# Residual behind layers 1 to 3: two of four column groups turned by VectorE and in-SBUF transfers instead of TensorE

## What is computed

```python
for i in range(DEPTH):
    hn = rmsnorm(x, norm_g[i])
    y = mixer[i % 3](hn, w_in, ..., w_out)   # proj = h @ w_in ... o @ w_out
    x = x + y
return rmsnorm(x, final_g)
```

## Time and profile before

| | |
|---|---|
| runs | 1754.71, 1755.09, 1756.72 us |
| span of the profiled execution | 1753.0 us (the page gives no device time of that execution by itself; the span lies 2.1 us under the median run) |
| PE, matmuls | 1743.7 us busy, 99% |
| DVE | 1146.3 us, 65% |
| ACT | 912.2 us, 52% |
| DMA queue of SP | 64.5% of 16 engines |
| granted TensorE clock | 0.999 mean |
| adds of `xres`, groups 0 and 1 behind layer 1 | at 432.17 and 438.22 us of the span |
| the same behind layers 2, 3 and 4 | 761.07 and 767.12; 1228.19 and 1234.24; 1699.07 and 1705.12 us |

### The profile page before, as it was taken

The page is one execution under the profiler, slowest core; times in us unless marked ns, Lnnn a source line. Parts: engine busy times, 40 slices in busy tenths (PEclk is TensorE's granted clock), DMA queues, the critical chain, the costliest instruction groups (busy, mean ns, idle before and its releaser), DMA issues.

```text
span 1753.0 us, 25040 instructions
## 1 busy us (share of the span) xinstructions
PE 1743.7 (99%) x8282; PEld 1457.9 (83%) x8282; DVE 1146.3 (65%) x1902; ACT 912.2 (52%) x1424; POOL 40.2 (2%) x99
## 2 busy tenths in 40 slices
PE   9999999999999999999999999999999999999998
PEld 7888888888888888888888888888888888888887
DVE  7766666665558888865655565655666666666655
ACT  7554545454556666645544444454545445454543
POOL 1000000000000000000000000000000000000000
PEclk9999999999999999999999999999999999999999
DMA  8666565655565555457997699866566666656563
GB/s 281 180 179 180 169 183 173 183 167 192 181 185 164 159 156 156 152 180 166 170 164 209 175 166 179 210 172 189 182 188 175 178 178 174 184 169 181 171 212 131
DMA packets 171301, 313.16 MB, mean 179 GB/s; under 512 B 10871, under 2 KB 27837, under 8 KB 171101
## 3 DMA queue, kind: packets, MB, share of 16 engines
q1 hardware_dynamic: 170800, 311.54, 64.5%
q0 software_dynamic: 48, 0.13, 0.2%
q10 hardware_dynamic: 380, 0.56, 0.1%
HBM read 310.10 MB, written 2.10 MB: 178 GB/s over the span
## 4 chain that ended last, share of the span: by engine, by line
PE 99%; DMA 0%; issue 0%; DVE 0%; ACT 0%; SPq 0%; POOLq 0%; POOL 0%; DVEq 0%
PE acc L962 30%; PE acc L964 30%; PE acc L963 30%; PE tp L927 4%; PE sc L963 1%; PE sc L962 1%; PE sc L964 1%; PE sc L994 0%; DMA xres<-in_x_dram 0%; PE sc L1052 0%; PE sc L1050 0%; PE sc L1051 0%; PE sc L1033 0%; PE sc L1032 0%; PE tp L962 0%
## 5 line engine op out<-in xcount | busy, mean ns | idle before, releaser
L1781 DVE TENSOR_TENSOR w_lo<-raw,w_hi 128x1024 fp32r<-128x1024 f32 x583 | 707.8, 1223 | 457.4 <-ACT w_hi L899 456.1
L899 ACT ACTIVATE w_hi<-raw 128x1024 fp32r<-128x1024 f32 x583 | 613.5, 1059 | 451.1 <-PE acc L964 445.0
L962 PE MATMUL acc<-w_hi,xt_hi 128*128 128x512 f32 x1824 | 719.5, 394 | 0.0
L964 PE MATMUL acc<-w_hi,xt_lo 128*128 128x512 f32 x1824 | 711.4, 390 | 0.0
L963 PE MATMUL acc<-w_lo,xt_hi 128*128 128x512 f32 x1824 | 710.3, 389 | 0.0
L964 PEld LDWEIGHTS acc<-w_hi,xt_lo 128*128 128x128 f32 x1824 | 342.3, 188 | 72.6
L963 PEld LDWEIGHTS acc<-w_lo,xt_hi 128*128 128x128 f32 x1824 | 342.8, 188 | 65.8
L962 PEld LDWEIGHTS acc<-w_hi,xt_hi 128*128 128x128 f32 x1824 | 342.6, 188 | 65.6
L962 PE MATMUL acc<-w_hi,ot_hi 128*128 128x512 f32 (+1 forms) x520 | 202.5, 390 | 0.0
L964 PE MATMUL acc<-w_hi,ot_lo 128*128 128x512 f32 (+1 forms) x520 | 200.9, 386 | 0.0
L963 PE MATMUL acc<-w_lo,ot_hi 128*128 128x512 f32 (+1 forms) x520 | 200.7, 386 | 0.0
(11 more groups left out here) (289 smaller groups left out, 1145.6 us busy)
## 6 DMA issues: line engine op xcount, KB each, us to landing
raw<-in_da_w_in_dram SPq DMA_DIRECT2D x255, 512.0 KB, 3.7
raw<-in_ml_w_in_dram SPq DMA_DIRECT2D x96, 512.0 KB, 5.3
raw<-in_sw_w_in_dram SPq DMA_DIRECT2D x72, 512.0 KB, 3.7
raw<-in_da_w_out_dram SPq DMA_DIRECT2D x64, 512.0 KB, 3.7
raw<-in_sw_w_out_dram SPq DMA_DIRECT2D x32, 512.0 KB, 3.6
raw<-in_ml_w_in_dram SPq DMA_DIRECT2D x64, 256.0 KB, 4.8
raw<-in_ml_w_out_dram SPq DMA_DIRECT2D x32, 512.0 KB, 3.8
xres<-in_x_dram SPq DMA_DIRECT2D x3, 512.0 KB, 8.9
```

What stands on the lines that cost most here:

```text
L899: act.activation(w_hi[:, q:q + 2, :], raw[:, 2 * p:2 * p + 2, :], ACT.Copy).then_inc(hi_ready, 1)
L962: pe.matmul(out_ap, k_hi, m_hi, start=start, stop=False)
L964: return pe.matmul(out_ap, k_lo, m_hi, start=False, stop=stop)
L1781: dve.tensor_tensor(w_lo[:, two, :], raw[:, two, :], w_hi[:, q:q + 2, :].bitcast(F32), ALU.subtract).then_inc(lo_ready, 1)
```

## The change

For groups 0 and 1 behind layers 1 to 3 PE makes no transposes. DVE, right behind the add, transposes the group in blocks of 32x32 with one instruction (128x1024 elements). SP then moves each block to its place among the partitions: 16 transfers of 32 partitions x 1 KB for a group, four at each of four slots (22 to 25 for group 0, 24 to 27 for group 1), behind that slot's weight load, the first ones after a wait for the transpose. ACT and DVE split the group from SBUF at slots 24 and 26 instead of 20 and 22 from PSUM. Buffers `th`, `qs`, `gs` and part of `scr`, which stand idle there, are used. The table `X_SPLIT` holds for layer 4 too. Groups 2 and 3 and the start stay as they are.

```diff
-X_SUM, X_TURN, X_SPLIT, X_END = (18, 20, 27, 3), (16, 18, 25, 1), (20, 22, 29, 5), (14, 16, 24, 32)
+X_SUM, X_TURN, X_SPLIT, X_END = (18, 20, 27, 3), (16, 18, 25, 1), (24, 26, 29, 5), (14, 16, 24, 32)
+X_MOVE, X_MOVED = (22, 24), 2
...
+        x_blocks = [scr_flat[:, 4 * BLK:4 * BLK + T * JW].rearrange("p (t j n) -> p t j n", t=T, j=4),
+                    gs[:].rearrange("p t (j n) -> p t j n", j=4)]
+        x_moved = [th[:].rearrange("p t (j n) -> p t j n", j=4), qs[:].rearrange("p t (j n) -> p t j n", j=4)]
+
+        def x_chunk(n, c):
+            return (th, qs)[n][:].rearrange("p t (j k n) -> p (t j) k n", j=4, k=4)[:, :, c, :]
...
+            def move_x(l, idx):
+
+                for n in range(X_MOVED):
+                    q = idx - X_MOVE[n]
+                    if l == NL - 1 or not 0 <= q < 4:
+                        continue
+                    if q == 0:
+                        sp.wait_ge(sig["x_turned"], in_out(l, "x_turned", n + 1))
+                    for j in range(4):
+                        sp.dma_start(x_moved[n][32 * j:32 * j + 32, :, q, :], x_blocks[n][32 * q:32 * q + 32, :, j, :])\
+                          .then_inc(sig[f"x{n}_moved"], 16)
...
                     sp.dma_start(raw[:, 2 * s:2 * s + 2, :], rows_of[:, :, JW * n:JW * n + JW]).then_inc(raw_full[s], 16)
+                    move_x(l, q)
...
+                if l >= 0 and n < X_MOVED:
+                    act.wait_ge(sig[f"x{n}_moved"], in_out(l, f"x{n}_moved", 256))
+                    for c in range(4):
+                        at = KC * (l + 1) + 4 * n + c
+                        dst = xt_hi[:, 4 * n + c, :].rearrange("p (j n) -> p j n", n=32)
+                        act.activation(dst, x_chunk(n, c), ACT.Copy, scale=gcol[:, at:at + 1]).then_inc(sig["t_hi"], 1)
+                    return
...
                     if w.first_job_of_layer:
-                        pe.wait_ge(free[name], in_out(w.l - 1, name, 3 if p == 0 else 4))
+                        pe.wait_ge(sig["x_lo"], in_out(w.l - 1, "x_lo", X_MOVED))
+                        pe.wait_ge(free[name], in_out(w.l - 1, name, (3 if p == 0 else 4) - X_MOVED))
...
-                if (ln := w.x_due(X_TURN)) is not None:
+                if (ln := w.x_due(X_TURN)) is not None and ln[1] >= X_MOVED:
...
+                if l >= 0 and n < X_MOVED:
+                    dve.wait_ge(sig[f"x{n}_moved"], in_out(l, f"x{n}_moved", 256))
+                    for c in range(4):
+                        at = KC * (l + 1) + 4 * n + c
+                        lo, hi = (buf[:, 4 * n + c, :].rearrange("p (j n) -> p j n", n=32)
+                                  for buf in (xt_lo, xt_hi[:].bitcast(F32)))
+                        if c % 2 == 0:
+                            dve.wait_ge(sig["t_hi"], in_out(l, "t_hi", 4 * n + c + 2))
+                        op = dve.scalar_tensor_tensor(lo, x_chunk(n, c), gcol[:, at:at + 1], hi, ALU.mult, ALU.subtract)
+                    op.then_inc(sig["x_lo"], 1)
+                    return
...
+                if l < NL - 1 and n < X_MOVED:
+
+                    wait_emptied(dve, l, OUT0[l] + n)
+                    dve.transpose(x_blocks[n].rearrange("p t j (k n) -> p t k j n", n=32),
+                                  xres[:, :, JW * n:JW * n + JW].rearrange("p t (k j n) -> p t k j n", k=4, j=4))\
+                       .then_inc(sig["x_turned"], 1)
```

More of the change, by code:

```diff
@@ L79 @@
     "t_hi":      ((0, 0, 16), (0, 4, 16), (0, 2, 16), (0, 4, 16)),
+    "x_turned":  ((0, 0, 0), (0, 0, 2), (0, 0, 2), (0, 0, 2)),
+    "x0_moved":  ((0, 0, 0), (0, 0, 256), (0, 0, 256), (0, 0, 256)),
+    "x1_moved":  ((0, 0, 0), (0, 0, 256), (0, 0, 256), (0, 0, 256)),
+    "x_lo":      ((0, 0, 0), (0, 0, 2), (0, 0, 2), (0, 0, 2)),
     "x_sq":      ((0, 0, 8), (0, 0, 8), (0, 0, 8), (0, 0, 8)),
@@ L369, in build, with x_tp @@
         vs_row, gs_row = scr_flat[0:8], gs[0:8].rearrange("p t n -> p (t n)")
+        x_blocks = [scr_flat[:, 4 * BLK:4 * BLK + T * JW].rearrange("p (t j n) -> p t j n", t=T, j=4),
[3 more added lines that the diff above has]
+            return (th, qs)[n][:].rearrange("p t (j k n) -> p (t j) k n", j=4, k=4)[:, :, c, :]
+        def x_tp(l, n):
+            return in_out(l, "tp_0", n if l < 0 else n - X_MOVED), in_out(l, "tp_1", n if l < 0 else n - X_MOVED)
         RUN = T * (PAD + P)
@@ L653, in x_half_turned_hi @@
                 cols = [gcol[:, at + c2:at + c2 + 1] for c2 in range(2)]
-                turned_hi(lambda c: xt_hi[:, 4 * n + c, :], b, f"tp_{b}", in_out(l, f"tp_{b}", n), cols)
+                turned_hi(lambda c: xt_hi[:, 4 * n + c, :], b, f"tp_{b}", x_tp(l, n)[b], cols)
             act.dma_start(rows[0:64, :], norm_g.rearrange("l (c p) -> (l c) p", p=P)).then_inc(gains_in, 16)
@@ L944, in x_turn @@
             def x_turn(l, n):
-                if l < NL - 1:
-                    turn_eight(lambda t: xres[:, t, JW * n:JW * n + JW], [in_out(l, f"tp_{b}", n) for b in range(2)])
+                if l < NL - 1 and not (l >= 0 and n < X_MOVED):
+                    turn_eight(lambda t: xres[:, t, JW * n:JW * n + JW], x_tp(l, n))
             pe.wait_ge(consts, 1)
@@ L1335, in x_half_turned_lo @@
                 turned_lo(lambda c: xt_lo[:, 4 * n + c, :], lambda c: xt_hi[:, 4 * n + c, :].bitcast(F32), b, f"tp_{b}",
-                          in_out(l, f"tp_{b}", n), [gcol[:, at + c2:at + c2 + 1] for c2 in range(2)],
+                          x_tp(l, n)[b], [gcol[:, at + c2:at + c2 + 1] for c2 in range(2)],
                           in_out(l, "t_hi", 4 * n + 2 * b))
```

## The result

The changed kernel took 1766.69 us (median, 1766.14 to 1768.83), the kernel before 1755.14 beside it: ratio 1.0066, 95% interval 1.0054 to 1.0078. It is slower by 0.66%, where a gain of 5.4 us was forecast; 1766.7 lies above the range. The rival that came true is C, SP's run of issues, at a smaller size than it was priced, and with a second loss that no case of the prediction had.

What follows compares the result with a forecast made beforehand. PE was taken to bound the kernel, with the new chain hidden in ACT's and DVE's lead: six turns of 0.90 us, 5.4 us, off 1755.1 give 1749.7 us. Range 1748.8 to 1753.5 us.

Steps and rivals of the forecast that it cites:

- C: SP's 37 issues in a row behind each boundary become the bound from 0.56 us each; 1788 us at 0.87; chance 0.07.
- What bounds the kernel: PE, busy 99% of the span with two waits, both in the start; six turns removed at 0.90 us give 5.4 us.
- DVE's transpose: Right behind the add of slot 18: 1.23 us, hidden in DVE's idle time up to 2.45 us.
- splits from SBUF: ACT's splits of groups 0 and 1 at slots 24 and 26: 1.57 us each, against 1.55 from PSUM.
- the two final gains of layer 4: DVE at slots 24 and 26: 1.37 us each, less than its 1.50 us wait for ACT per slot, cost 0.
- I take 0.48: SP's run from slot 22 on: issues start 0.48 us apart, so group 1's last move is issued at 452.1.
- 1.1 us to spare: Slot 27 behind layer 1, the tightest place: `w_lo` ready at 464.8, PE wants it at 465.9.
- Landing: Moves land 3.7 us after issue, like weight loads: group 0 at 449.1, group 1 at 455.8.
- The lead: ACT and DVE are 5.6 us ahead of PE's need at each slot; 4.5 of it is used.
- The clock: PE around the turns kept for groups 2 and 3: granted clock stays 1.00, the 2.4 GHz level, with no idle PE.
- B: Blocks come late at the three boundaries and part of the gain is given back: 1752.3 or 1753.9 us; chance 0.14.
- Rival D: PE's matmuls slow through added SBUF traffic, or the transposes filled time lost anyway: no change, 1755.1 us; chance 0.06.

Runs made afterwards that it cites:

- the unused moves: The kernel before, PE's turns and split slots kept, plus DVE block transposes and SP's 96 moves with results not used: 1755.11 us, ratio 1.0001.

## Why the prediction was wrong, step by step

- **What bounds the kernel: right.** PE has no slack and the turns are worth 0.90 us each; 5.4 us came out in two kernels that keep the whole change (1749.71 and 1749.79 against the 1749.7 forecast).
- **DVE's transpose: right**, 1.25 us for 1.23, hidden. Adds, splits from SBUF (1.71 against 1.57) and the two final gains of layer 4: right, that boundary moved by 0.0.
- **SP: this step failed.** The term "I take 0.48" for the spacing of the issues came from stores to HBM; an issue from SBUF to SBUF costs 0.64 with its gap, and so does nearly every weight load between them. Over 36 steps that is 36 x 0.16 = 5.8 us, more than the 1.1 us to spare. I had taken 0.50 as the upper bound; the nearest row was of another kind, and the bound should have reached as far as the slow issues of the earlier trace rows, which I had given to a rival alone.
- **Landing: mis-sized the other way**, 2.1 instead of 3.7, which gave 1.6 back; the estimate of 2.1 that the prediction draws from the Trainium skill ("DMA: Bandwidth & Descriptors", Anatomy of one DMA) came out here, although that section is on transfers that GpSimd issues and these were SP's. Some irregular issues (one of 1.5 us) took another 1: group 1 was there at 460.9, 5.1 late. What makes single issues long is not shown.
- **The lead: right.** With 1.1 to 1.3 us to spare, 5.1 late makes 3.8 to 4.0 of stall; the runs give 11.2 us for three, 3.7 each.
- **The clock: missing.** Rivals B and C counted a stall at its own length. A stall of 3.7 us cost on average 1.9 more at each boundary. The prediction looked at the clock only for the case in which PE would not stop.
- **Rival C**: mechanism, place and turning point (issues of 0.56) were right. By its formula an issue of 0.64 gives 3.1 us of stall with the real landing, 1755.1 + 3 x (3.1 - 1.8) = 1759.0. The clock adds 5.8; the 1.9 us that are left are stall beyond 3.1 us, for the most part the irregular issues. Its price of 1788 was for 0.87. A chance of 0.07 was too little for a margin of 1.1 us that hung on 36 times an unknown.
- **Rival D**: the unused moves show that the traffic costs nothing.

## What to carry to other kernels

When many small transfers are issued in a row, the issue price times their number is a term of the sum, and it needs a row of the same kind (both ends in SBUF); if there is none, take the bound from the worst row. Put the wait for a late block behind the work that the critical engine wants next, not in front of it: the same lateness cost 17.0 us at one slot (1766.69 against 1749.71), about 1 us one slot later, and nothing three slots later. And price a stall of TensorE of several us with the clock that it loses, about half as much again here.

## What the runs showed of the hardware

- The issue of a 32 KB move holds SP for 0.43 us with HBM as the source and for 0.60 to 0.62 from SBUF to SBUF, nearly whatever the runs (64 of 512 bytes, 32 of 1 KB) and the partitions (32, 128). On GpSimd the move within SBUF takes 0.54.
- The issue of a 512 KB weight load out of HBM takes 0.37 us alone, 0.42 behind moves out of HBM, and 0.59 to 0.61 behind moves within SBUF.
- 32 KB from SBUF to SBUF land 2.1 to 2.5 us after the issue in the median (1.8 to 3.6 singly), and 3.3 to 3.6 when two engines issue at once.
- DVE transposes 128x1024 f32 in blocks of 32x32 in 1.25 us, as long as a two-input operation of that size (1.23).
- With idle times of 3.45 to 3.65 us went a half clock of 3.4 to 6.8 us, which began as early as 1.4 us before PE resumed and as late as 1.4 us after; with waits of 0.4 us it did not come, nor where useless matmuls filled the time.
